# Prompt attention: keys kept negated with the row minimum taken, queries read in place, compressed values stacked once

## The reference

```
def masked_softmax(s, mask):
    s = jnp.where(mask, s, NEG)
    m = jnp.max(s, axis=-1, keepdims=True)
    p = jnp.where(mask, jnp.exp(s - m), 0.0)
    return p / jnp.maximum(jnp.sum(p, axis=-1, keepdims=True), 1e-30)
...
    s = jnp.einsum('btgpd,bsgd->btgps', q, kv[..., 0, :]).astype(jnp.float32) * SCALE
    s = s - slopes[None, None, :, :, None] * dist[None, :, None, None, :]
    p = masked_softmax(s, mask[None, :, None, None, :])
    return jnp.einsum('btgps,bsgd->btgpd', p.astype(kv.dtype), kv[..., 1, :])
...
    o = (gates[:, :, 0, :, :, None] * o_c + gates[:, :, 1, :, :, None] * o_s
         + gates[:, :, 2, :, :, None] * o_w)
```

## Time and profile before

| what | value |
|---|---|
| median of 3 runs | 936.3 us (934.24 to 938.38) |
| the profiled execution: its own time | 931.72 us |
| its span in the profile | 929.9 us |
| PE busy | 838.3 us, 90% of the span |
| DVE, ACT, POOL busy | 440.6, 334.5 and 122.4 us |
| `prompt` in the trace | from 227.5 to 332.9 us of the span |

### The profile page before, as it was taken

One profiled execution on the slowest core, in us unless ns is written; L12 is line 12 of the kernel. 1 busy time (PEld: TensorE's weight loads), 2 busy tenths in 40 slices (PEclk: granted clock), 3 DMA queues, 4 the chain that ended last, 5 costly groups with the idle time before them and its releaser, 6 DMA issues.

```text
span 929.9 us, 16973 instructions
## 1 busy us (share of the span) xinstructions
PE 838.3 (90%) x7066; PEld 757.7 (81%) x7066; DVE 440.6 (47%) x971; ACT 334.5 (36%) x608; POOL 122.4 (13%) x119
## 2 busy tenths in 40 slices
PE   5999988877777787898899999999999999999994
PEld 4999966764544454566899999999999999999993
DVE  5335545645677756663535543244333442343324
ACT  6501054542355555453424441123211331133203
POOL 0000101100486424441020000000000000000000
PEclk8999999997699978999899999999999999999998
DMA  8912636841254020556420222222112222222002
GB/s 286 333 51 92 189 75 219 278 147 60 77 183 136 2 80 4 223 227 151 145 89 2 91 90 91 90 90 79 50 56 86 90 90 90 90 90 90 0 0 102
DMA packets 48782, 102.72 MB, mean 110 GB/s; under 512 B 7498, under 2 KB 19166, under 8 KB 46429
## 3 DMA queue, kind: packets, MB, share of 16 engines
q1 hardware_dynamic: 41821, 68.48, 22.2%
q0 software_dynamic: 6912, 33.56, 10.4%
HBM read 97.62 MB, written 8.53 MB: 114 GB/s over the span
## 4 chain that ended last, share of the span: by engine, by line
PE 50%; DVE 1%; ACT 1%; issue 0%; DVEq 0%; ACTq 0%
PE bank L1987 50%; DVE low L1974 1%; ACT low L1900 0%; DVE wl L1913 0%; PE bank L2029 0%; ACT wh L1856 0%; ACT small L1906 0%; DVE small L1971 0%; DVE hT L1926 0%; DVE hT L1951 0%; DVE xl L1930 0%; ACT low L1870 0%; DVE xl L1919 0%; ACT xh L1872 0%; DVEq L1810 0%
## 5 line engine op out<-in xcount | busy, mean ns | idle before, releaser
L1987 PE MATMUL bank<-xh,wh 128*128 128x288 f32 x640 | 138.2, 298 | 4.3 <-DVE xl L1919 3.9
L1987 PE MATMUL bank<-xl,wh 128*128 128x288 f32 x640 | 138.0, 297 | 0.0
L1987 PE MATMUL bank<-xh,wl 128*128 128x288 f32 x640 | 137.9, 297 | 0.0
L1856 ACT ACTIVATE wh<-low 128x1024 fp32r<-128x1024 f32 x72 | 75.1, 1050 | 121.3 <-PE bank L1987 121.0
L1987 PE MATMUL bank<-ah,wl 128*128 128x288 f32 x512 | 109.7, 296 | 0.0
L1987 PE MATMUL bank<-ah,wh 128*128 128x288 f32 x512 | 109.6, 296 | 0.0
L1987 PE MATMUL bank<-al,wh 128*128 128x288 f32 x512 | 109.6, 296 | 0.0
L1987 PEld LDWEIGHTS bank<-xh,wh 128*128 128x128 f32 x640 | 104.0, 190 | 5.0 <-DVE wl L1913 4.2
L1987 PEld LDWEIGHTS bank<-xl,wh 128*128 128x128 f32 x640 | 104.1, 190 | 0.0
L1987 PEld LDWEIGHTS bank<-xh,wl 128*128 128x128 f32 x640 | 103.9, 190 | 0.0
L1951 DVE TENSOR_TENSOR hT<-bank,hT 128x288 f32<-128x288 f32 x64 | 26.3, 453 | 138.9 <-PE bank L1987 138.9
(11 more groups left out here) (323 smaller groups left out, 1375.2 us busy)
## 6 DMA issues: line engine op xcount, KB each, us to landing
low<-in_w_up SPq DMA_DIRECT2D x8, 2048.0 KB, 8.2
low<-in_w_down SPq DMA_DIRECT2D x8, 2048.0 KB, 7.8
zone<-in_cmp_w SPq DMA_DIRECT2D x16, 256.0 KB
o_swin<-in_state_win SPq DMA_DIRECT2D x8, 504.0 KB
px<-in_x_prompt SPq DMA_DIRECT2D x4, 512.0 KB, 5.4
u_raw<-in_w_in SPq DMA_DIRECT2D x1, 2048.0 KB, 10.0
q_raw<-in_w_in SPq DMA_DIRECT2D x1, 2048.0 KB, 10.4
low<-in_state_win SPq DMA_DIRECT2D x4, 512.0 KB
```

What stands on the lines that cost most here:

```text
L1856: act.activation(wcols(m.wh, i), raw_cols(i), ACT.Copy).then_inc(wh_ready, 1)
L1987: last = pe.matmul(out(i, hf), w[wi], half(x[:, k, :], hf), start=first and part == 0, stop=end and part == 2)
```

## The change

- ACT's copy of the turned prompt keys (L891) gets a factor of -1, so the scores arrive negated; the penalties get a second factor of -1; the fused instruction takes the minimum in place of the maximum, which is already the negated maximum, and the exponential gets a factor of -1. L1199 and its semaphore `summed` go: ACT and PE wait for the fused instruction itself.
- `stage_queries` goes with `qst`; PE reads the head's queries from `qT`, and its waits for `q_staged` go.
- `stage_values` goes. One instruction in the opening writes `vst` for all four heads (64 partitions x 512 columns, both inputs in SBUF).
- The loops over heads on ACT and DVE are written out.

```diff
-            act.activation(m.kT[:, br, 0:SEQ], pb[5 + br][:, :], ACT.Copy).then_inc(kt_kept, 1)
+            act.activation(m.kT[:, br, 0:SEQ], pb[5 + br][:, :], ACT.Copy, scale=-1.0).then_inc(kt_kept, 1)
...
                     last = act.activation(m.cp[v % 4][:, g, 0:width(v)], m.cp[v % 4][:, g, 0:width(v)], ACT.Exp,
-                                          bias=nm(v)[:, g:g + 1], accum_out=su(v)[:, g:g + 1])
+                                          bias=nm(v)[:, g:g + 1], scale=-1.0, accum_out=su(v)[:, g:g + 1])
...
-            with act.Fori(0, HPG - 1) as j:
-                body(j, False)
-            body(HPG - 1, True)
+            for j in range(HPG):
+                body(j, j == HPG - 1)
...
-                dve.tensor_copy(m.qst[:, a:a + SEQ // 2], m.qT[:, bass.ds(j, 1), a:a + SEQ // 2]
-                                .rearrange("p a t -> p (a t)")).then_inc(q_staged, 1)
...
                     last = dve.tensor_scalar(m.pre[:, g, :], const(m, "negd"),
-                                             const(m, "slopes")[:, bass.ds(j + HPG * g, 1)], None, ALU.mult)
+                                             const(m, "slopes")[:, j + HPG * g:j + HPG * g + 1], -1.0, ALU.mult,
+                                             ALU.mult)
...
                     last = dve.tensor_tensor_reduce(m.cp[v % 4][:, g, 0:w], m.pre[:, g, SEQ - w:SEQ],
-                                                    pb[2 * (v % 2) + g][:, 0:w], 1.0, -3e38, ALU.add, ALU.max,
+                                                    pb[2 * (v % 2) + g][:, 0:w], 1.0, 3e38, ALU.add, ALU.min,
                                                     nm(v)[:, g:g + 1])
-                last.then_inc(summed, 1)
-                dve.wait_ge(summed, j * U + (v + 1))
-                dve.tensor_scalar(nm(v), nm(v), -1.0, None, ALU.mult).then_inc(smax, 1)
+                last.then_inc(smax, 1)
...
                     if not last and u == AHEAD - 1:
-                        stage_queries(j + 1, 0)
                         stage_penalties(j + 1)
-                    if not last and u == AHEAD:
-                        dve.wait_ge(scored, j * U + U)
-                        stage_queries(j + 1, 1)
-                if not last:
-                    dve.wait_ge(o_done, j + 1)
-                    stage_values(j + 1)
...
-            stage_values(0)
-            with dve.Fori(0, HPG - 1) as j:
-                body(j, False)
-            body(HPG - 1, True)
+            heads_first = [64, HPG, NKV, HD]
+            dve.tensor_tensor(m.vst[0:64].rearrange("p j (g d) -> p j g d", g=NKV),
+                              m.vrep[0:64, :].rearrange("p (g d) -> p g d", g=NKV).unsqueeze(1).broadcast_to(heads_first),
+                              const(m, "hmask")[0:64, :].rearrange("p (g j) -> p j g", g=NKV).unsqueeze(3)
+                              .broadcast_to(heads_first), ALU.mult).then_inc(vst_staged, 1)
+            for j in range(HPG):
+                body(j, j == HPG - 1)
...
-                if v % U in (0, 4):
-                    pe.wait_ge(q_staged, (j + v // U) * 2 + (1 + (v % U) // 4))
                 if v >= 2:
-                    pe.wait_ge(summed, j * U + (v - 1))
+                    pe.wait_ge(smax, j * U + (v - 1))
                 for g in range(2):
                     a = HD * g
-                    last = pe.matmul(pb[2 * (v % 2) + g][:, 0:w], m.qst[a:a + HD, P * i:P * i + P],
+                    last = pe.matmul(pb[2 * (v % 2) + g][:, 0:w], m.qT[a:a + HD, j + v // U, P * i:P * i + P],
                                      m.kT[a:a + HD, branch(v), 0:w], start=True, stop=True)
```

More of the change, by code:

```diff
@@ L275, in place_attention @@
     m.pre = at(w + 6144, 2, 512)
-    m.qst, m.ccT, m.cc = at(w + 7168, 512), at(w + 7680, 512), at(w + 8192, 256)
-    m.vrep, m.vst, m.kc2 = at(w + 8448, P), at(w + 8576, P), at(w + 8704, 16)
+    m.vst, m.ccT, m.cc = at(w + 7168, HPG, P), at(w + 7680, 512), at(w + 8192, 256)
+    m.vrep, m.kc2 = at(w + 8448, P), at(w + 8704, 16)
     m.kst = [at(w + 512 * s, 512) for s in range(3)]
@@ L1083, in prompt @@
     ident = const(m, "ident")
-    q_staged, pre_ready, vst_staged = sem("q_staged"), sem("pre_ready"), sem("vst_staged")
-    scored, summed, smax, exped, rec, scl_ready = (
-        sem("scored"), sem("summed"), sem("smax"), sem("exped"), sem("rec"), sem("scl_ready"))
+    pre_ready, vst_staged, rec = sem("pre_ready"), sem("vst_staged"), sem("rec")
+    scored, smax, exped, scl_ready = sem("scored"), sem("smax"), sem("exped"), sem("scl_ready")
     scaled, p_turned, kept_act, kept_dve = sem("scaled"), sem("p_turned"), sem("kept_act"), sem("kept_dve")
@@ L1144, in body @@
                         act.wait_ge(o_done, j + 1)
-                        act.activation(m.mixT[:, bass.ds(j, 1), 0:SEQ].rearrange("p a t -> p (a t)"), pb[6][:, :],
+                        act.activation(m.mixT[:, j, 0:SEQ], pb[6][:, :],
                                        ACT.Copy).then_inc(o_kept, 1)
@@ L1194, in sums @@
                     last = dve.tensor_tensor_reduce(m.cp[v % 4][:, g, 0:w], m.pre[:, g, SEQ - w:SEQ],
[L1195 removed]
+                                                    pb[2 * (v % 2) + g][:, 0:w], 1.0, 3e38, ALU.add, ALU.min,
                                                     nm(v)[:, g:g + 1])
[L1197 to L1199 removed]
+                last.then_inc(smax, 1)
             def factors(j, v):
                 dve.wait_ge(exped, j * U + (v + 1))
+                a = NH * (1 + branch(v))
+                gt = m.gates[:, tile(v), a:a + NH].rearrange("p (g h) -> p g h", g=2)[:, :, j + v // U]
                 dve.reciprocal(su(v), su(v)).then_inc(rec, 1)
                 dve.wait_ge(rec, j * U + (v + 1))
[L1206 to L1208 removed]
+                dve.tensor_tensor(su(v), su(v), gt, ALU.mult).then_inc(scl_ready, 1)
             def keep_turned(j, v):
@@ L1237, in _ @@
             last.then_inc(kc_ready, 1)
-            for part in range(2):
-                stage_queries(0, part)
             dve.tensor_tensor(cc4, const(m, "cmpd").rearrange("p (i n) -> p i n", n=PBLK).unsqueeze(2)
@@ L1320, in values @@
                 if u == 0:
-                    pe.wait_ge(o_kept, j + 1)
-                if u == 1:
-                    pe.wait_ge(vst_staged, j + 1)
+                    if j:
+                        pe.wait_ge(o_kept, j)
                 out = lambda g: pb[6][HD * g:HD * g + HD, P * i:P * i + P]
@@ L1332, in values @@
                     for g in range(2):
-                        last = pe.matmul(out(g), m.vst[0:64, HD * g:HD * g + HD], m.ccT[0:64, P * i:P * i + P],
+                        last = pe.matmul(out(g), m.vst[0:64, j, HD * g:HD * g + HD], m.ccT[0:64, P * i:P * i + P],
                                          start=False, stop=True, skip_group_check=True)
```

6 lines of the change are left out of this document (removed).

## The result

The changed kernel takes 925.2 us (median of 20 runs, 920.0 to 930.8) against 932.7 for the kernel before (20 runs, 927.0 to 938.4, the forecast's three among them): a ratio of 0.9925, 95% interval 0.9904 to 0.9946. Most of the 5.1, 3.6, is the median of three runs that the forecast started from: 936.3, against 932.7 over twenty runs and 933.2 to 934.5 in the four later groups of 17 to 35. The ratios leave out the runs that lie over 1.5% above the fastest of their kernel; the medians count all runs.

A forecast was written before the change was run, and what follows sets the result against it. `prompt` was taken as bounded by waits round a ring of DVE's copy, PE's `values` and `turn`, no engine being full; 2.3 + 1.4 + 1.9 + 0.4 = 6.0 us off 936.3 gives 930.3, range 927.0 to 934.0.

The forecast's parts named there:

- the 5.1: How many us the forecast's absolute time, 930.3, lay above the measured 925.2.
- The stacked values, 2.3: Passages between heads: without `stage_values` the copy of step 1 starts earlier, by 0.94, 0.77 and 0.61 us; sum 2.3.
- Penalties and queries, 1.4: Ahead of step 5's copy, heads 0 to 2: no query copy and earlier penalties save 1.3 to 1.6 us, taken as 1.4.
- the negations, 1.9: Negations dropped: 0.6 at step 6, 0.8 at step 3, 0.2 at head 3's step 5, 0.3 at head 2's end.
- At nothing: Priced at 0: factors of -1, the penalties' second factor, minimum for maximum, instruction fetch of the written-out loops.
- The opening, 0.4: Start of `prompt`: `values(0, 0)` 0.7 us earlier, half of it lost to PE's half clock; taken as 0.4.
- The lock: In the opening, the stacking instruction with two SBUF operands waits for POOL's third multiply, costing up to 1.3 us.
- the first rival: Opening: stacking isn't held by POOL, `values(0, 0)` starts 2.0 us earlier; gain 7.6 to 9, about 928; 15%.
- if the rise stays where it is: Opening: if PE's clock rise stays in place, 0.7 us more work runs at half clock and half is lost.
- The rival in which PE's ring absorbs more: Only the passages between heads and half of the rest stay, 2.3 + 1.0; gain 3.3 us, 933; 27%.
- The minimum: The 64 fused instructions: forecast at 0 cost; a rival had the minimum form slower than the maximum, 942; 4%.
- the locks pass from the negation to the gate multiply: Rival: the gate multiply takes over the locks, and PE's clock falls a window more; gain 0 to 2, 935.5; 4%.

The follow-up runs named there:

- e7: The changed kernel with nine products of 512 columns added in PE's waits (four, then five), results unused; ratio 0.9935 to the kernel before.
- e5: The kernel before with only the loops over heads written out on ACT and DVE; ratio 0.9973 to the kernel before.
- e6: The changed kernel with the stacking instruction reading the values from PSUM, so one SBUF operand; ratio 0.9906 to the kernel before.
- e10: The changed kernel with stacking read from PSUM and moved earlier, two penalty buffers, four added PE products; 922.3 us, ratio 0.9870 to the kernel before.

## Why the prediction was right or wrong

The terms of the sum, priced by the two traces:

**The stacked values, 2.3: right.** Over the last interval of a head and the first of the next, the passage into head 2 gave 0.82 (0.77 forecast), that into head 3 0.93 (0.61, and 0.3 of the negation's). That into head 1 lay at half clock and lost 0.62; in e7, where the clock was full, it gave 1.04, for 0.94.

**Penalties and queries, 1.4, and the negations, 1.9: right in sum, not in shape.** Steps 4 to 6 together gave 0.84, 0.72 and 0.73 in heads 0, 1 and 2, where 1.4 and the 0.6 of step 6 were forecast: 2.3 for 2.0. Steps 2 and 3 gave 0.99 for 0.8 over the four heads, head 3's step 5 0.21 for 0.2. But step 6 gave back 0.30 where I had booked a gain of 0.2, and steps 4 and 5 gave more to make up for it: `values` of step 6 still waits for ACT, which copies behind the second exponential.

**At nothing: right.** The fused instructions keep their length, 0.68 with 512 columns, and the penalties take 0.64 on average, against 0.62. In e5 the written-out loops lengthened no full-clock interval of the table by more than 0.01 but step 6's, by 0.11; no stall for the fetch of instructions shows.

**The opening, 0.4: wrong in size.** `values(0, 0)` came 2.75 earlier. From the traces: scores start 0.83 earlier; they take 1.99 instead of 3.39, 1.40; the compressed products 3.74 instead of 4.34, 0.60; 0.59 between these and the compressed copy, where the negations stood; the stacking 0.67 longer. The sum, 0.83 + 1.40 + 0.60 + 0.59 - 0.67, is 2.75. The lock was there and is shown by e6, so this is not the first rival, whose gain stood on its absence. What I had missed is that the rows of the first scores were themselves rows at half clock. The windows of before (first row) and e7 around them, and of the changed kernel just ahead of its own:

```profile
221.13:231.34 10.21, 7.97 (x48) 5.25 (x48) 5.37 (x14) 0.98 (x2) 0.11 (x1) 0.50 0.26 88
215.18:225.40 10.22, 8.56 (x48) 5.33 (x48) 5.82 (x15) 1.03 (x2) 0.11 (x1) 0.50 0.21 74
223.74:230.55 6.81, 5.10 (x40) 4.06 (x40) 3.37 (x6) 1.38 (x3) 0.00 (x0) 0.50 0.00 0
```

The step reads "if the rise stays where it is, 0.7 us more of the work is done at that level": I had looked at the half clock behind the scores and not at the one under them. In before it had begun 6.4 us ahead of `prompt`, so the wait for the copies did not bring it about; at most it kept the clock from rising, as it rose in the changed kernel 0.7 ahead of `prompt`. And e7 has the same long stretch without the wait. So 0.83 of the 2.75 is the wait itself; whether the 2.0 of the clock (1.40 + 0.60) belong to the change or to the execution stays open. Part was paid back: the next half-clock stretch reached 1.6 us further into head 0 (0.80 lost there) and another lay across the passage into head 1. And 0.52 at the very end of `prompt` is no gain of the change: the profile of before had half clock there. With it the parts of this section add up to 7.1, for the 7.0 between the traces.

That 6.0 came near 7.0 is partly luck: the opening and the passage into head 1, forecast at 0.4 + 0.94, gave 2.75 - 0.80 - 0.62 = 1.33, the same sum out of three terms of the clock that were not in it.

**The failed step of the absolute number** is "the same 6.0 off 936.3 gives 930.3". Three runs, 934.2 to 938.4, of a kernel whose runs go from 926 to 944 are no base to 0.4%. Against 932.7 the same 6.0 gives 926.7, 1.5 from the 925.2 measured, and the same gains of 2.3 to 9.3 give 923.4 to 930.4, which holds it; the range had room for the unknown costs and none for the base. The one row that lay against it, the profiled execution at 931.72, I named and didn't use.

The rival in which PE's ring absorbs more had a real mechanism, step 6, but not its size. The minimum costs nothing that shows (0.68 with 512 columns in either form). That the locks pass from the negation to the gate multiply was seen in the opening: 0.70 for 0.16.

## What to carry to other kernels

Before a saving is taken off a median, ask how far the runs scatter and how many there are. Here half-clock stretches of PE fall differently from one execution to the next; an interval between two fixed instructions gets round them, a total does not. Read the granted clock of every row that a sum is built on, and how far back that stretch reaches: a wait in front of a slow burst need not be what slowed it. Where a DVE instruction with two SBUF operands meets a busy POOL, read one of them from PSUM if the data is there.

## What the runs showed of the hardware

A DVE instruction of 512 columns took 0.67 with one operand in PSUM and 2.06 with both in SBUF, started 0.03 us apart from the same POOL multiply of 1.47. Even the gate multiply of 2 columns waits for POOL's end so: 0.70 instead of 0.16. The Trainium skill (page "SBUF — State Buffer", section "Who interferes with whom") has it that a DVE instruction with two SBUF inputs contends with a GpSimd instruction that reads SBUF. The traces agree, with 2.06 against 0.67.

Four or nine products more in PE's waits ended the half-clock stretch of the opening at 12.5 and 13.9 of the stage, instead of 20.5 to 27.6, and head 0 from `values(0, 0)` on took 19.0 and 19.2 (e10, e7); in the other traces it took 20.3 to 22.4.

Unedited kernels, profiled again, had PE at half clock over different stretches: the stage ahead of `prompt`, the same in all kernels but for the factor in two key copies, took 221 to 234 us. What decides where the stretches fall I have not found.
